# Second attention of a two-block transformer, stepped by query tile instead of by turn

## What is computed

```
for block of 128 queries:                       # forgetting attention
    s = q . k * scale + F[t] - F[s]; mask s > t
    y_fox = softmax(s) . v
for block of 128 queries:                       # indexer attention
    iscore = sum_h w[t,h] * relu(q_idx . k_idx); keep the top 128 keys <= t
    logits = q . k * scale + bias[bucket(t - s)]; only kept keys
    y_dsa = softmax(logits) . v
merged = sigmoid(gate_fox) * (y_fox @ w_fox) + sigmoid(gate_dsa) * (y_dsa @ w_dsa)
```

## Time and profile before

| | |
|---|---|
| median of three runs | 1390.85 us (1390.78 to 1392.7) |
| the profiled execution | 1392.73 us, its span 1390.9 us |
| PE busy | 1364.6 us (98%) |
| DVE, ACT, POOL busy | 818.7, 517.0, 561.8 us (59, 37, 40%) |
| mean granted TensorE clock | 0.994 |
| the eight passes | about 710 to 872 us of the span |

### The profile page before, as it was taken

How to read it: one execution, slowest core, us unless ns; L and a number is a source line. 1 busy time by engine, 2 the same in 40 slices (tenths; PEclk the granted TensorE clock), 3 DMA queues, 4 the chain that set the end, 5 groups by cost and what they waited for, 6 DMA issues and landing times.

```text
span 1390.9 us, 18371 instructions
## 1 busy us (share of the span) xinstructions
PE 1364.6 (98%) x6358; PEld 1104.4 (79%) x6358; DVE 818.7 (59%) x1074; ACT 517.0 (37%) x794; POOL 561.8 (40%) x230
## 2 busy tenths in 40 slices
PE   7999999999999999999999999999999999999997
PEld 6777787888888888887777777888878888888886
DVE  4455577574765746885988866334554343352474
ACT  4333224331422314234356665322345323142233
POOL 3334245353553545424322223443525535345361
PEclk9999999999999999989999999999999999999999
DMA  7643234366383763623522232333422423323221
GB/s 206 143 84 91 77 106 140 86 191 173 111 236 96 219 184 106 197 55 106 77 73 60 82 92 79 104 91 92 138 74 91 132 80 108 89 88 118 81 91 61
DMA packets 216323, 156.66 MB, mean 113 GB/s; under 512 B 8996, under 2 KB 197792, under 8 KB 216136
## 3 DMA queue, kind: packets, MB, share of 16 engines
q1 hardware_dynamic: 215800, 154.62, 39.8%
q10 hardware_dynamic: 464, 1.27, 0.3%
HBM read 151.13 MB, written 4.74 MB: 112 GB/s over the span
## 4 chain that ended last, share of the span: by engine, by line
PE 50%; DVE 2%; ACT 1%; issue 0%; POOL 0%; ACTq 0%; DVEq 0%
PE ps L551 28%; PE ps L998 12%; PE ps L947 3%; PE ps L886 2%; PE ps L863 1%; PE ps L850 1%; PE ps L836 1%; PE ps L837 1%; DVE work L2069 1%; DVE work L2066 0%; PE ps L840 0%; DVE work L2051 0%; DVE top L2049 0%; DVE sel L2054 0%; POOL w_lo L511 0%
## 5 line engine op out<-in xcount | busy, mean ns | idle before, releaser
L511 POOL TENSOR_TENSOR w_lo<-raw,w_hi 128x1024 fp32r<-128x1024 f32 x222 | 558.4, 2524 | 795.1 <-ACT w_hi L1045 790.3
L551 PE MATMUL ps<-u_hi,w_hi 128*128 128x512 f32 x1016 | 411.4, 405 | 6.8 <-POOL w_lo L511 2.3
L551 PE MATMUL ps<-u_hi,w_lo 128*128 128x512 f32 x1016 | 398.5, 392 | 0.0
L551 PE MATMUL ps<-u_lo,w_hi 128*128 128x512 f32 x1016 | 398.3, 392 | 0.0
L1045 ACT ACTIVATE w_hi<-raw 128x1024 fp32r<-128x1024 f32 x221 | 231.3, 1053 | 247.8 <-PE ps L998 91.0
L551 PEld LDWEIGHTS ps<-u_hi,w_hi 128*128 128x128 f32 x1016 | 193.3, 190 | 48.9 <-issue 5.4
L551 PEld LDWEIGHTS ps<-u_hi,w_lo 128*128 128x128 f32 x1016 | 192.1, 189 | 41.2
L551 PEld LDWEIGHTS ps<-u_lo,w_hi 128*128 128x128 f32 x1016 | 192.8, 190 | 39.2 <-issue 1.9
L551 PE MATMUL ps<-y_hi,w_hi 128*128 128x512 f32 x320 | 126.7, 396 | 0.1
L551 PE MATMUL ps<-y_lo,w_hi 128*128 128x512 f32 x320 | 124.6, 389 | 0.0
L551 PE MATMUL ps<-y_hi,w_lo 128*128 128x512 f32 x320 | 124.6, 389 | 0.0
(11 more groups left out here) (268 smaller groups left out, 1771.9 us busy)
## 6 DMA issues: line engine op xcount, KB each, us to landing
raw<-w_in SPq DMA_DIRECT2D x69, 512.0 KB, 3.8
raw<-w_mlp SPq DMA_DIRECT2D x64, 512.0 KB, 3.8
adaw<-w_ada SPq DMA_DIRECT2D x32, 768.0 KB, 4.6
raw<-w_up SPq DMA_DIRECT2D x32, 512.0 KB, 6.2
raw<-w_down SPq DMA_DIRECT2D x32, 512.0 KB, 6.5
raw<-w_out SPq DMA_DIRECT2D x16, 512.0 KB, 4.0
bias_rows<-fbrow SPq DMA_DIRECT2D x4, 640.0 KB
xtok<-x SPq DMA_DIRECT2D x4, 512.0 KB, 6.4
```

The source lines that it names most:

```text
L511: pool.tensor_tensor(w_lo[:, s, :], raw[:, s, :], w_hi[:, s, :], ALU.subtract).then_inc(lo_ready[s], 1)
L551: last = pe.matmul(ps[0:cols, bank, :], w[:, s, c], r[:, k, :], start=(k == ks[0] and w is w_hi and r is r_hi), stop=(k == ks[-1] and w is ...
```

## The change

Only PE's order in the passes changes. The loop goes over query tiles: the turns of both heads, the scores of both heads of the tile two further on, then (at tile 0) the values of tiles 2 and 3 of the pass before or (at tile 2) those of tiles 0 and 1 of this pass, then two pieces, twelve projection matmuls, in one run. No instruction is added or taken away, and DVE, ACT, POOL and the DMA queues keep their order.

```diff
             for p in range(2 * NQ):
-                for n in range(8):
-                    if n == 1 and p > 0:
+                for i in range(NT):
+                    for n in (2 * i, 2 * i + 1):
+                        t_step(p, n)
+                    for n in (2 * i, 2 * i + 1):
+                        coming = 8 * p + n + LOOK
+                        if coming < 16 * NQ:
+                            s_step(coming // 8, coming % 8)
+                    if i == 0 and p > 0:
                         pv(p - 1, 2)
                         pv(p - 1, 3)
-                    if n == 5:
+                    if i == 2:
                         pv(p, 0)
                         pv(p, 1)
-                    t_step(p, n)
-                    coming = 8 * p + n + LOOK
-                    if coming < 16 * NQ:
-                        s_step(coming // 8, coming % 8)
-                    pieces.pop(0)()
+                    for _ in range(2):
+                        pieces.pop(0)()
```

## The result

The change makes the kernel slower by 0.3%: **1395.19 us** (median of 11 runs, 1393.0 to 1396.77) against 1391.07 (11 runs, 1389.57 to 1392.7) for the kernel before on the same chip, ratio 1.003 with a 95% interval of 1.0021 to 1.0039. The forecast was 1391.4 us, a change of less than 0.2%; the measured time lies outside the range of 1388.0 to 1394.7. The profiled execution of the change spans 1393.9 us; the one of before spanned 1390.9.

What follows compares the result with a forecast made beforehand. PE was taken to bound the passes, DVE next with 2.76 us idle. PE's work +0.15, start +0.2, nearer wait +0.4, shrinking key wait -0.2 gave +0.55 us on 1390.85: 1391.4 us, range 1388.0 to 1394.7.

Steps and rivals of the forecast that it cites:

- The wait that comes near: Next pass's scores of head 1 against step 7's logits: just fits in passes 1 to 4, +0.2 us each in 5 and 6.
- the list of turns: Head 1's turns in the new order: 0.18 us per pass lost for steps 3 and 7, 0.06 for steps 1 and 5.
- The rival for "slower" (POOL): POOL takes the turn of DVE's weight scaling, DVE 2.1 us later, PE waiting about 1.1 us per pass; chance 0.14.
- PE's work: PE's own matmul work in the new order: +0.02 us per pass, +0.15 over the 7.25 passes behind the start.
- the lower bound of -0.22: PE's work per pass if values behind a mask matmul cost nothing beyond the usual 0.04 us.
- The values behind a mask matmul: Values start 0.16 us behind a mask matmul's start, 0.12 later: 0.24 us per pass lost for two.
- The start: Pass 0, where DVE holds PE: the new order costs +0.2 us, not the 1.6 of the longer wait.
- The wait ahead of step 5's scores: In pass 0 PE idles 2.8 us for the logits of step 3, where it waited 1.19 before.
- the 0.7 us ahead of pass 1's scores: At the end of pass 0, head 1's scores wait for step 7's logits, ending at 723.17: another 0.7 us idle.
- The next pass's scores: Head 1's scores of the coming pass wait for step 7's logits in passes 5 and 6: +0.2 us each, +0.4.
- The wait for keys: Pass 4's wait of 0.5 us for the next pass's keys shrinks, since that group arrives later: -0.2 us.
- Rival 2: The clock falls in pass 0's long wait to about half speed: +1.1 us, 1392.5; chance 0.16.

Runs made afterwards that it cites:

- e1: The change with a second PSUM bank for head 1's turns: 1391.86 us, ratio 0.9998 to the kernel before.
- e7: The change with two banks for head 1's turns and, at the start, DVE's logits of step 3 ahead of a round: 1390.5 us, ratio 0.9994.
- e11: The change with two banks, early logits of step 3, and the output scaling of passes 5 to 7 behind step 7's logits: 1390.89 us, ratio 0.9998.
- e2: The change with one bank, ACT copying step 7's turns ahead of the last two query halves instead of behind: 1400.62 us, ratio 1.007.
- e4: The kernel before with only tile 0 of every pass in the new order: 1395.31 us, ratio 1.0026.
- e3: The change with tile 0 of every pass in the old order, tiles 1 to 3 as changed: 1394.09 us, ratio 1.0016.
- e6: The kernel before with a second bank for head 1's turns and nothing else: 1391.72 us, ratio 1.0001.
- e12: The change with one bank and only DVE's logits of step 3 earlier at the start: 1395.19 us, ratio 1.0029.

## Why the prediction was wrong

**The step that failed** is "The wait that comes near". It says of each thing that the new order asks for earlier whether its partner is done, and looked at one: the next pass's scores of head 1. Moving step 1's turns ahead of a piece and a values block was priced as PE work only (0.06 and 0.18 in the list of turns), never set against the bank that these turns write. `t_step` waits for `probt_ready1` as well as for `att_prob`. The wait was known, since the description of the turns ahead of the prediction names it, but it stood at nothing in the sum without a reason. The runs: with the second bank the kernel is 0.3 us above the kernel before of its group, where the change is 4.1 above its own, so the bank is worth 3.8 us, and passes 1 to 6 give 3.77; with one bank the new order of tile 0 alone costs 3.7 (1391.57 to 1395.31), of which 2.65 lie in passes 1 to 6. The rival for "slower" (POOL) had the sign but another mechanism: in the change the scaling takes over 2 us in pass 4 alone, as before.

**PE's work.** Forecast +0.02 us per pass, measured -0.21 (19.46 in e1 and e7 against 19.67), close to the lower bound of -0.22 but for other reasons. The values behind a mask matmul cost what I took, 0.16 from start to start. In the change:

```profile
743.14 0.23 PE L842 MATMUL ps<-causalb,identb 128*128 128x128 bf16 x1
743.30 0.32 PE L863 MATMUL ps<-probt_even,vtoks 128*64 128x128 f32 x1
```

The turns were mis-sized: in pass 2 they cost 1.86 us in e1 (0.14, 0.36, 0.57 and 0.79 for 2, 4, 6 and 8) against 1.78 before, +0.08 where I had +0.24. Before, step 4's three turns took 0.37 instead of 0.24, because the scores behind them waited for keys that DVE finished at 761.52:

```profile
760.83 0.69 DVE L2125 TENSOR_TENSOR k_both<-ps,k_both 64x512 fp32r<-64x512 f32 x1
```

```profile
761.25 0.49 PE L850 MATMUL ps<-small,prob_evens 128*128 128x128 f32 x3
761.62 0.30 PE L836 MATMUL ps<-k_both,q_up 128*128 128x128 f32 x1
```

In the new order these scores come three turns later, and the 0.13 us, a wait that no list of waits shows, are gone. (That it was a wait is read from these times, not tried.) A further 0.07 is the pace of a run: the twelve take 2.84 or 2.87 us, two runs of six took 1.47 each, 1.56 ahead of values.

**The start.** The wait ahead of step 5's scores was 2.59 us (2.8 forecast), and step 6's turns came 16.79 us behind the first turn against 16.54 before (726.64 and 709.85): +0.25 where I had +0.2. Pass 0 as a whole is 0.25 longer. That is right, but one of its steps is not: the 0.7 us ahead of pass 1's scores did not come. PE had lost 0.7 us from start to start at tile 1, by the wait of 0.53 for the bank, and so reached these scores (722.54) just as the logits of step 7 ended (722.48). In pass 0 the missed wait took the place of a forecast one and cost nothing.

**The next pass's scores.** In passes 5 and 6 they wait 0.28 us each (0.32 from start to start where 0.04 is free); I had 0.2. Right, and e11 shows that `final_norm` is the cause. Pass 4 is 0.2 shorter, as forecast (20.42 against 20.62), but by luck. The wait for keys did not shrink, it went altogether, and the wait for the bank stands in the change instead. In e1, without that one, PE waits 0.32 us for the logits of step 7, although the prediction says that in passes 1 to 4 it just fits:

```profile
801.51 0.33 PE L836 MATMUL ps<-k_both,q_up 128*128 128x128 f32 x1 [0.32 <-DVE mneg L2091]
```

The scalings of 2.7 us in this pass may be why it does not; no run here tries it.

**The sum, by its own steps.** Without the missed wait passes 1 to 6 take 119.02 us (e1) against 119.37 before, -0.35; pass 7 gives -0.02 and the start +0.25. That is -0.1 us, 0.7 below the forecast's +0.55. The missed wait adds 3.77, which makes the 3.66 of the region.

**Rival 2** is real, though the change's own profile does not show it. Of the four profiles with this wait (the change, e1, e2, e4) three show windows of 0.50 to 0.54 behind it. Its price is about 0.9 us: e1's pass 0 took 22.02 and e4's 22.09 where the change took 21.15 without it, and I had 1.1. How often it comes in the timed runs stays open, since only one execution of each kernel was profiled. The Trainium skill, TensorE: Matmul & The Clock Gate, Part 1, says that the chip's monitoring period runs free of the kernel, so that the same gap can meet it differently; that agrees with these rows.

**The bound** "passes 1 to 3 shorter than 19.4 or longer than 20.0" was crossed in all three: 20.32, 20.03, 20.03.

## What to carry to other kernels

When instructions are moved together, list for each of them every wait that it carries, the one for a free output buffer too, and compare the old slack of each (here 2.65 us) with the work that is taken from in between (3.6 us). This says that there will be a wait, not how long it is: 3.6 less 2.65 is 1.0, and 0.54 was lost, because the copy itself came 0.6 us earlier in the pass. A wait that never ended last shows in no list of waits, so read it from the partner's end and the user's start. And a cure that moves work on one engine (e2) can cost more than the illness, through two others that only just missed each other; another buffer (e1) changed no engine's order.

## What was not expected of the hardware

- A wait between turns costs more than the idle time listed: 0.37 us in the list are 0.54 from start to start, and 0.99 are 1.15 (832.45 to 833.71, less 0.11). This is a matter of reading and not of the chip: the list counts from the drawn end of the turn ahead, 0.27 behind its start, and the next turn could have started 0.11 behind it, which makes the 0.16.
- The last projections of a run of twelve stand 0.227 us apart (745.60 to 746.96 in six steps) where those of a run of six stood 0.23 apart. What makes it was not tried.
- A clock of half speed also came behind a chain of shorter waits: in e3 1.19, 0.58 and 1.11 us within 5.5 us, then

```profile
718.00:720.00 2.00, 2.00 (x7) 0.50 0.00 0
720.00:722.00 2.00, 2.00 (x8) 0.68 0.00 0
```

The kernel before has the first two of them (e6: 1.19 and 0.57) and stays at 1.00; with 1.64 and 1.11 (e12) it stays there too.
